# Two experts at fixed ranks, their weights issued before the ranking of the experts is known

## The chip, the cores and the metric

One core of one Trainium2 chip runs the whole program. The metric is the device time of one execution in microseconds (us). The kernel before took 2995.73 us (median of 3 runs, 2994.79 to 2996.75).

## The reference, cut to what matters

The program is two transformer blocks over 256 tokens of width 1024. The first has two layers of attention and a product-key expert lookup. The second mixes tokens with two recurrent mixers and ends in a mixture of experts (`_moe`), which is the only part that the change touches:

```
scores = sigmoid(xt @ w_router)                  # 256 tokens x 64 experts
biased = scores + bias;  keep the best 4 of 8 groups of 8 experts
sel = top_k(candidates, 8);  wts = scores[sel] / sum * 2.5
for each expert e, for the tokens that chose it:
    y += wts * ((silu(x @ w_gate[e]) * (x @ w_up[e])) @ w_down[e])
out = y + shared expert
```

There are 256 x 8 = 2048 assignments over 64 experts, 32 on average. Each expert has 3 MB of float32 weights: gate and up together are 1024 x 512, down is 256 x 1024.

## The kernel before, in words

All weights of all 64 experts are streamed through SBUF once, in 192 pieces of 1 MiB. An expert has three pieces: part 0 and part 1 are the two halves of gate and up, part 2 is down.

The experts are ranked by how many tokens chose them. VectorE builds a key (size x 64 plus 63 minus the number of the expert) and sorts the 64 keys with eight rounds of max8 and match-replace in `moe` (L1741 to L1746). From the sorted keys it makes the list of expert numbers, which is announced as `order` (L1751). An expert's rank decides how much room it gets: ranks 0 to 7 have 128 rows, ranks 8 to 31 have 64, ranks 32 to 63 have 32. Where a size is over its room, a flag is set (`over`, L1753 to L1757), and a second wave over the table `AGAIN` serves the rows that did not fit; without the flag every engine jumps over it.

`STEPS` (L249 to L258) is the first wave, 28 steps. A step fills the 128 rows of TensorE with one, two or four experts. Step 0 holds ranks 8 and 9, step 1 ranks 32 to 35, step 2 rank 0, step 3 ranks 10 and 11, and so on.

`PIECES` (L269) is the order of the 192 pieces: for each step s its part 0, its part 1, and then part 2 of the step before. So the order starts with step 0 part 0 (2 pieces), step 0 part 1 (2), step 1 part 0 (4), step 1 part 1 (4), step 0 part 2 (2), step 2 part 0 and part 1, step 1 part 2 (4), step 3 part 0. Below, piece n is the n-th of this order, counted from 0. There are 13 places in SBUF (`PLACES`); piece n goes to place n modulo 13.

SyncE issues the pieces, strictly in this order (`weights` in `sync_program`, L2652). It waits once for `order`, then reads each expert's number from the list with a value_load and issues the piece with a source address made from it. From piece 13 on it waits until the matmuls that used the place's former piece are done: `("used", "piece", step, part)` of piece n - 13. The first 13 have other conditions: pieces 0 to 5 wait for the last projection of the mixer, which was done long before, pieces 6 and 7 for the second half of the shared expert's up projection (`("ps", "shared", 1)`), pieces 8 and 9 for the end of the shared expert's down projection (`("used", "w_sh")`), and pieces 10 to 12 for the store of the token table. Ahead of piece 9 SyncE also issues the store of the shared expert's output to `y_tab`, and that waits for this output.

TensorE runs, in program order: router, shared up projection, sizes and ranks, tables of slots for 12 steps (`slots`), `shared_down`, and then `experts`. In `experts` (L956) the order is: up(0), turn(1), hidden(0); then for each s: up(s), one chunk of slot tables, turn(s+1), down(s-1), hidden(s). up(s) uses parts 0 and 1 of step s, down(s) uses part 2. So down(0) comes after up(1) and turn(2). GpSimd gathers the rows of each step from `x_tab` with one indirect DMA (L2502), and adds the results to `y_tab` with one indirect accumulating DMA per expert (L2514).

Of the kernel before, what the change touches and what calls it, by code (L numbers as in the profile page):

```python
# [5 lines left out]
P = 128  # L6
ALU = mybir.AluOpType
# [13 lines left out]
class Counts:  # L21
# [3 lines left out]
    def __init__(self):  # L25
        self.table, self.known = {}, False
# [134 lines left out]
def bc(a, axis, n):  # L161
    u = a.unsqueeze(axis)
    s = list(u.shape)
    s[axis] = n
    return u.to_broadcast(s)


def heads(a, n):
    return a.rearrange("p (h x) -> p h x", h=n)
# [79 lines left out]
def expert_steps():  # L249


    r = []
    for i in range(8):
        r += [(8 + 2 * i, 9 + 2 * i), tuple(range(32 + 4 * i, 36 + 4 * i)), (i,)]
    return r + [(24 + 2 * i, 25 + 2 * i) for i in range(4)]


STEPS = expert_steps()  # L258
CAPACITIES = ((0, 128), (8, 64), (32, 32))

AGAIN = [(r,) for r in range(32)] + [(8, 9)] + [tuple(range(32 + 4 * i, 36 + 4 * i)) for i in range(8)]
AGAIN_FROM = [128] * 8 + [64] * 24 + [192] + [32] * 8
WAVES = (STEPS, AGAIN)
FIRST = [[sum(len(x) for x in steps[:s]) for s in range(len(steps))] for steps in WAVES]
LAST_CHUNK = 6
PLACES = 13


PIECES = [[(t, part, i) for s in range(len(steps) + 1) for t, part in ((s, 0), (s, 1), (s - 1, 2))  # L269
           if 0 <= t < len(steps) for i in range(len(steps[t]))] for steps in WAVES]  # L270
PIECE_OF = [{x: n for n, x in enumerate(pieces)} for pieces in PIECES]


class MoeSide:


    def __init__(self, ar, modT, iu):
        two = lambda o, n: ar(o, n).rearrange("p (c n) -> p c n", c=2)
        self.Wt, self.sg, self.bi, self.Mk = (two(128 * i, 128) for i in range(4))
        self.g8, self.m8, self.kp = ar(512, 64), ar(576, 8), ar(584, 8)  # L280
        self.gsum, self.ssum, self.big = ar(592, 8), ar(600, 8), ar(608, 64)
        self.TW = ar(672, 256).rearrange("p (c e x) -> p c e x", c=2, x=2)
        self.RW, self.RWT, self.rkp = two(928, 256), two(1184, 256), two(1440, 128)
        self.Pm, self.key, self.order, self.rank, self.rev = (ar(1568 + 64 * i, 64) for i in range(5))
        self.ST = ar(1888, 128).rearrange("p (s x) -> p s x", x=2)
        self.ig, self.iy, self.colm = ar(2016, 64), ar(2080, 72), ar(2168, 1)
        self.OH = ar(2304, 2048).rearrange("p (c e s) -> p c e s", c=2, e=8)
        self.ysh = two(4352, 2048)
        self.xg = [ar(6400 + 1024 * i, 1024) for i in range(4)]
        self.XT, self.yb = ([ar(o + 1024 * i, 1024) for i in range(2)] for o in (10496, 12544))  # L290
        self.sgm, self.hid, self.hidT = ([ar(o + 256 * i, 256) for i in range(2)] for o in (14592, 15104, 15616))
        self.hsh = ar(15104, 512)
        self.sums = [two(6400, 2048), two(8448, 2048)]
        self.sh2 = modT[:, 24:32]
        self.row_of, self.add_to = iu[:, 0:64], iu[:, 64:132]
        self.digits, self.expert = iu[:, 192:256], iu[:, 256:320]


def build(nc, d, out):
    import numpy as np  # L300
    ctx = ExitStack()
    with ctx:
        def sb(name, n, dt=F32):
            return ctx.enter_context(nc.sbuf_tensor(name, [P, n], dt))
# [25 lines left out]
        iu = sb("iu", 512, U32)  # L330
# [4 lines left out]
        def tile_of(*name):  # L335

            return banks[where.get(name, 0)]
# [21 lines left out]
        def R(i, k):  # L359
            return ring[:, i * 1024:(i + k) * 1024]  # L360
# [18 lines left out]
        at = Counts()  # L379
# [25 lines left out]
        def piece(wave, *which):  # L405

            i = PIECE_OF[wave][which] % PLACES
            return R(2 * i, 2) if i < 10 else ar(16384 + 2048 * (i - 10), 2048)
# [7 lines left out]
        def tensor_program(pe):  # L416
# [451 lines left out]
            def moe():  # L868
# [81 lines left out]
                def slots_again():  # L950
                    b = fresh("slots", 1, 0, among=(0,))
                    for k, rs in enumerate(AGAIN):
                        one_hots(1, k, [k % 8], [k], [rs], b)
# [86 lines left out]
        def vector_program(v):  # L1040
# [660 lines left out]
            def moe():  # L1701
                m = moe_side
# [29 lines left out]
                for c in range(2):  # L1732
# [6 lines left out]
                          ("out", "rank", c))  # L1739
                    v.ts(m.RW[:, c, 0:64], m.RW[:, c, 0:64], 1000.0, None, ALU.add, None, ("RW", c))  # L1740
                v.stt(m.key, tile_of("sizes")[:, 0:64], 64.0, m.rev, ALU.mult, ALU.add, ("out", "sizes"))  # L1741
                for i in range(8):
                    o8 = m.order[:, 8 * i:8 * i + 8]
                    v.max8(o8, m.key)
                    if i < 7:
                        v.replace8(m.key, o8, m.key, -1.0)  # L1746
# [5 lines left out]
                v.ts(m.Pm, m.rank, m.colm, None, ALU.is_equal, None, ("permutation",))  # L1752
                for i, (rank, n) in enumerate(CAPACITIES):  # L1753
                    v.ts(m.ssum[:, i:i + 1], m.order[:, rank:rank + 1], 64.0 * (n + 1), None, ALU.is_ge, None)
                for i in (1, 2):
                    v.tt(m.ssum[:, 0:1], m.ssum[:, 0:1], m.ssum[:, i:i + 1], ALU.max)
                v.cp(flag[:, 0:1], m.ssum[:, 0:1], ("over",))  # L1757
                v.wait_ge(*at("ps", "by rank", 0))
# [14 lines left out]
                def rows(wave, g, o, n):  # L1773

                    part = slice(o, o + n)
                    v.wait_ge(*at("ps", "slots", wave, g))
                    v.cp(m.ST[:, part], tile_of("slots", wave, g)[:, 0:2 * n].rearrange("p (e x) -> p e x", x=2),
                         ("out", "slots", wave, g))
                    x, ig = m.ST[:, part, 0], m.ig[:, part]
                    v.ts(ig, x, 0.0, 1000.0, ALU.is_equal, ALU.mult)  # L1780
                    v.stt(ig, x, -1.0, ig, ALU.add, ALU.add)
                    v.cp(m.row_of[:, part], ig)
                    return ig

                sr = C("slot_rows")
# [22 lines left out]
                def slots_again():  # L1808
                    for k, (rs, first) in enumerate(zip(AGAIN, AGAIN_FROM)):
                        v.wait_ge(*(at("used", "onehot", 1, k - 8) if k > 7 else at("used", "onehot", 0, LAST_CHUNK)))  # L1810
                        by = len(rs)
                        for c in range(2):
                            o = m.OH[:, c, k % 8, :].rearrange("p (x s) -> p x s", x=by)
                            v.tt(o, bc(C("iota")[:, first:first + P // by], 1, by),
                                 bc(m.rkp[:, c, rs[0]:rs[0] + by], 2, P // by), ALU.is_equal, ("onehot", 1, k))
                    ig = rows(1, 0, 0, 41)
                    v.cp(m.iy[:, 0:32], ig[:, 0:32])
                    v.tt(m.iy[:, 32:34], sr[:, 0:2], ig[:, 32:33].to_broadcast([P, 2]), ALU.add)
                    v.tt(heads(m.iy[:, 34:66], 8), bc(ig[:, 33:41], 2, 4), bc(sr[:, 2:6], 1, 8), ALU.add)
                    v.cp(m.add_to[:, 0:66], m.iy[:, 0:66], ("slots", 1, 0))  # L1820

                def experts(wave, more):
                    steps = WAVES[wave]
# [59 lines left out]
                with v.e.If(over > 0):  # L1883
                    slots_again()
                    experts(1, iter(()))
                    v.wait_ge(*at("added", 1, len(AGAIN) - 1, 0))
                    v.fill(m.m8, 0.0)
# [667 lines left out]
        def sync_program(sp):  # L2555
# [89 lines left out]
            m = moe_side  # L2645
# [5 lines left out]

            def weights(wave, before):  # L2652

                sp.wait_ge(*at("order"))
                e = {}
                for n, (s, part, i) in enumerate(PIECES[wave]):
                    if wave == 0 and n == 9:
                        load(rows_of(y_tab[0:T, :]), m.ysh, s_tab, ("tables",),
                             after=[("out", "ysh", c, i) for c in range(2) for i in range(2)])
                    rank = WAVES[wave][s][i]  # L2660
                    if wave == 0 and n == 20:
                        load(hT_sb[:, 0:D], d["rows"][14:15, :].to_broadcast([P, D]), s_post, ("loaded", "ffn", "post"),
                             after=[("ps", "shared", 1)])
                    if part == 0:
                        e[rank] = sp.e.value_load(m.expert[0:1, rank:rank + 1], min_val=0, max_val=63) if at.known else 0
                    src = d["w_down"][bass.ds(e.pop(rank), 1), :, :] if part == 2 else \
                        d["w_gu"][bass.ds(e[rank], 1), :, 2048 * part:2048 * part + 2048]
                    old = [("used", "piece", wave, *PIECES[wave][n - PLACES][0:2])] if n >= PLACES else before(n)
                    load(piece(wave, s, part, i), src.rearrange("a p n -> (a p) n"), piece_sems[wave][n % PLACES],
                         ("loaded", "piece", wave, s, part, i), after=old)  # L2670
# [177 lines left out]
```

## Time and profile before

| | us |
|---|---|
| median of 3 runs | 2995.73 |
| the profiled execution, its own time | 2992.89 |
| span of the profiled execution | 2991.1 |
| first piece of expert weights issued | 2371.19 |
| last piece issued | 2925.00 |
| end of the span | 2991.1 |

Times inside the profile are us from the start of the span. The expert stage is the last 620 us. The page's line of DMA shares cuts the span in 40 slices of 74.8 us; slices 32 to 39 are this stage. PE is TensorE, DVE is VectorE, SP is SyncE.

### The profile page before, as it was taken

The numbers are of one execution on the slowest core, as the hardware profiler recorded it, in microseconds if no ns is written. First come the engines' busy times: TensorE is split into PE (matmuls) and PEld (weight loads), VectorE is DVE, ScalarE is ACT, GpSimd is POOL, SyncE is SP. The second block draws the span as 40 slices with busy tenths as digits, with TensorE's granted clock in tenths as the row PEclk, the third lists the DMA queues.
The fourth block names the chain that finished last, engine by engine and source line by source line (L and its number), as shares of the span: only waits on it lengthen the run. The fifth ranks groups of instructions, "written<-read, shape, count | busy, mean of one in ns | idle before, by whom it ended". The sixth has DMA issues, their size and how long they took to land.

```text
span 2991.1 us, 29479 instructions
## 1 busy us (share of the span) xinstructions
PE 2436.7 (81%) x9692; PEld 1331.3 (45%) x9692; DVE 1598.9 (53%) x3289; ACT 836.0 (28%) x2272; POOL 830.9 (28%) x723
## 2 busy tenths in 40 slices
PE   7898888888887988998897899789797786767673
PEld 3684333333333766344443455458783532222221
DVE  4556657485444636758889877556644521121111
ACT  1313333333332412343343444323110111111110
POOL 1004333343331102334444556112010112122221
PEclk9799999999999799999999999899998788888887
DMA  7029999999998126999898899612113399999994
GB/s 276 1 85 403 422 422 422 422 415 422 422 398 346 57 85 248 376 366 395 355 420 313 358 422 395 245 43 71 43 57 131 140 408 397 389 391 381 382 381 147
DMA packets 129843, 885.95 MB, mean 296 GB/s; under 512 B 23184, under 2 KB 23568, under 8 KB 31760
## 3 DMA queue, kind: packets, MB, share of 16 engines
q0 software_dynamic: 86976, 553.74, 46.0%
q1 hardware_dynamic: 42704, 330.22, 27.5%
q8 instruction: 79, 1.29, 0.2%
q14 instruction: 84, 0.69, 0.1%
HBM read 877.56 MB, written 37.75 MB: 306 GB/s over the span
## 4 chain that ended last, share of the span: by engine, by line
PE 46%; DMA 25%; DVE 20%; ACT 4%; issue 3%; SPq 1%; POOL 1%; DVEq 0%; ACTq 0%; POOLq 0%
PE ps L155 44%; DMA ring<-in_peer_uv,idx_u 11%; DMA ring<-in_w_gu 6%; DVE ring L1307 6%; DVE arena L76 5%; DMA ring<-in_w_down 3%; ACT arena L125 3%; PE ps L158 2%; DMA arena<-in_w_gu 2%; DMA arena<-in_w_down 1%; DVE arena L1307 1%; DVE iu L113 1%; DVE arena L109 1%; SPq L2560 1%; DVE arena L97 1%
## 5 line engine op out<-in xcount | busy, mean ns | idle before, releaser
L155 PE MATMUL ps<-ring,arena 128*128 128x512 f32 (+3 forms) x3264 | 1262.9, 653 | 281.2 <-ACT arena L125 159.9
L155 PEld LDWEIGHTS ps<-ring,arena 128*128 128x128 f32 (+2 forms) x3264 | 473.6, 180 | 957.3 <-issue 605.1
L1307 DVE CUSTOM_DVE_ANT_0 ring<-ring,h 128x1024 f32<-128x1024 f32 x448 | 563.0, 1257 | 328.3 <-DMA ring<-in_peer_uv,idx_u 294.9
L2377 POOL DMA_INDIRECT ring<-in_peer_uv,idx_u x448 | 491.5, 1097 | 754.8 <-PE ps L155 609.4
L155 PE MATMUL ps<-arena 128*128 128x128 f32 (+7 forms) x2504 | 502.8, 383 | 106.4 <-ACT arena L125 42.9
L125 ACT ACTIVATE arena<-arena 128x1 f32<-128x1 f32 (+4 forms) x1097 | 296.7, 270 | 747.6 <-DVE arena L1307 646.3
L155 PEld LDWEIGHTS ps<-arena 128*128 128x128 f32 (+3 forms) x2504 | 316.0, 193 | 263.5 <-issue 148.3
L76 DVE TENSOR_TENSOR arena<-arena,ps 128x512 f32<-128x512 f32 (+1 forms) x158 | 93.7, 593 | 446.9 <-ACT arena L125 358.6
L125 ACT ACTIVATE arena<-ps 128x512 f32<-128x512 f32 (+4 forms) x198 | 109.8, 554 | 774.1 <-PE ps L155 712.5
L155 PE MATMUL ps<-ring,hT 128*128 128x512 f32 (+2 forms) x896 | 307.0, 503 | 16.9 <-DVE hT L97 11.9
L125 ACT ACTIVATE arena<-cst,arena 128x128 f32<-128x128 f32 x512 | 205.5, 401 | 162.3 <-PE ps L155 122.0
L155 PEld LDWEIGHTS ps<-ring,hT 128*128 128x128 f32 x896 | 171.7, 198 | 141.2 <-issue 114.1
L2514 POOL DMA_INDIRECT y_tab<-arena,iu x64 | 100.1, 1564 | 435.5 <-DVE arena L97 309.6
L134 POOL TENSOR_TENSOR small<-small,cst 128x1 f32<-128x1 f32 (+3 forms) x42 | 46.6, 1109 | 534.4 <-DVE small L84 520.6
L155 PE MATMUL ps<-hT,ring 128*128 128x128 f32 (+1 forms) x1280 | 182.2, 306 | 12.0 <-ACT hT L125 12.0
L155 PEld LDWEIGHTS ps<-hT,ring 128*128 128x128 f32 x1280 | 171.1, 199 | 21.1 <-issue 10.5
L158 PE MATMUL ps<-cst,arena 128*128 128x128 f32 (+1 forms) x706 | 114.9, 313 | 57.4 <-DVE arena L76 29.0
L158 PEld LDWEIGHTS ps<-cst,arena 128*128 128x128 f32 (+1 forms) x706 | 94.3, 158 | 112.8 <-issue 45.5
L97 DVE COPY arena<-ps 128x512 f32<-128x512 f32 (+5 forms) x102 | 59.6, 584 | 149.9 <-PE ps L155 81.5
L134 POOL TENSOR_TENSOR arena<-arena,cst 128x512 f32<-128x512 f32 (+2 forms) x52 | 67.6, 1301 | 230.8 <-DVE arena L76 135.4
L2377 POOL DMA_INDIRECT arena<-in_peer_uv,idx_u x64 | 70.6, 1103 | 130.7 <-PE ps L155 128.2
L1307 DVE CUSTOM_DVE_ANT_0 arena<-arena,h 128x1024 f32<-128x1024 f32 x64 | 81.1, 1267 | 42.4 <-DMA arena<-in_peer_uv,idx_u 36.5
(117 smaller groups left out, 1486.6 us busy)
## 6 DMA issues: line engine op xcount, KB each, us to landing
ring<-in_w_gu SPq DMA_DIRECT2D x98, 1024.0 KB, 28.5
ring<-in_w_down SPq DMA_DIRECT2D x52, 1024.0 KB, 29.8
ring<-in_w_in SPq DMA_DIRECT2D x16, 2048.0 KB, 12.6
arena<-in_w_gu SPq DMA_DIRECT2D x30, 1024.0 KB
ring<-in_w_mod SPq DMA_DIRECT2D x12, 2048.0 KB
ring<-in_peer_wq SPq DMA_DIRECT2D x8, 2048.0 KB, 8.1
ring<-in_w_o SPq DMA_DIRECT2D x6, 2048.0 KB, 11.1
ring<-in_w_gates SPq DMA_DIRECT2D x12, 1024.0 KB, 4.9
```

The costliest lines, as they stand in the source:

```text
L76: self.done(self.e.tensor_tensor(o, a, b, op), *names)
L97: self.done(self.e.tensor_copy(o, a), *names)
L109: self.done(self.e.max(out=o, in_=a), *names)
L113: self.done(self.e.max_index(o, m, a), *names)
L125: self.done(self.e.activation(o, a, f, **k), *names)
L134: self.done(self.e.tensor_tensor(o, a, b, op), *names)
L155: return self.e.matmul(o, lhsT, rhs, start=start, stop=stop, skip_group_check=True)
L158: return self.e.transpose(o, src, ident)
L1307: v.done(v.e.tensor_tensor_reduce(out=row, in0=row, in1=h[:, n // 128, :], scale=1.0, scalar=0.0, op0=ALU.mult, op1=ALU.add, accum_out=aa[ ...
L2377: g.e.indirect_dma_start(out=landing(n), out_offset=None, in_=d["peer_uv"], in_offset=bass.IndirectOffsetOnAxis(ap=idx_u[:, n:n + 1], axis ...
L2514: g.e.indirect_dma_start(out=y_tab, out_offset=index(m.add_to, n), in_=m.yb[s % 2], in_offset=None, bounds_check=2 * T - 1, oob_is_err=Fal ...
L2560: sp.e.dma_start(o, src).then_inc(sem, 16)
```

## The change

Experts 0 and 1 get ranks 8 and 9 whatever their sizes, and the others are ranked around them. The first round of the sort sees key -1 for both; ahead of the second round their keys return, raised by 65536 and 32768, so that they come first among what is left. The raise does not touch the low six bits, from which the expert's number is read. The room check looks at rank 10 in place of rank 8, and at the larger size of the two fixed experts. The table of the second wave gets two more entries. SyncE issues the six pieces of step 0 with constant addresses and waits for `order` only ahead of the first piece whose expert it has to read. In `PIECES` part 2 of step 0 moves from behind step 1 to places 4 and 5 of the order. The list of places and the condition of each piece number stay as they are.

```diff
-CAPACITIES = ((0, 128), (8, 64), (32, 32))
+KNOWN = {8: 0, 9: 1}
+CAPACITIES = ((0, 128), (10, 64), (32, 32))
...
+PIECES[0] = PIECES[0][0:4] + [(0, 2, 0), (0, 2, 1)] + [x for x in PIECES[0][4:] if x[0:2] != (0, 2)]
 PIECE_OF = [{x: n for n, x in enumerate(pieces)} for pieces in PIECES]
...
+                v.cp(m.kp[:, 0:2], m.key[:, 0:2])
+                v.fill(m.key[:, 0:2], -1.0)
                 for i in range(8):
                     o8 = m.order[:, 8 * i:8 * i + 8]
+                    if i == 1:
+                        for e in range(2):
+                            v.ts(m.key[:, e:e + 1], m.kp[:, e:e + 1], 32768.0 * (2 - e), None, ALU.add, None)
                     v.max8(o8, m.key)
...
-                for i in (1, 2):
+                v.tt(m.ssum[:, 3:4], m.kp[:, 0:1], m.kp[:, 1:2], ALU.max)
+                v.ts(m.ssum[:, 3:4], m.ssum[:, 3:4], 64.0 * 65, None, ALU.is_ge, None)
+                for i in (1, 2, 3):
                     v.tt(m.ssum[:, 0:1], m.ssum[:, 0:1], m.ssum[:, i:i + 1], ALU.max)
...
             def weights(wave, before):
-                sp.wait_ge(*at("order"))
...
-                    if part == 0:
+                    known = wave == 0 and rank in KNOWN
+                    if known:
+                        which = slice(KNOWN[rank], KNOWN[rank] + 1)
+                    elif part == 0:
+                        sp.wait_ge(*at("order"))
                         e[rank] = sp.e.value_load(m.expert[0:1, rank:rank + 1], min_val=0, max_val=63) if at.known else 0
-                    src = d["w_down"][bass.ds(e.pop(rank), 1), :, :] if part == 2 else \
-                        d["w_gu"][bass.ds(e[rank], 1), :, 2048 * part:2048 * part + 2048]
+                    if not known:
+                        which = bass.ds(e[rank] if part < 2 else e.pop(rank), 1)
+                    src = d["w_down"][which, :, :] if part == 2 else d["w_gu"][which, :, 2048 * part:2048 * part + 2048]
                     old = [("used", "piece", wave, *PIECES[wave][n - PLACES][0:2])] if n >= PLACES else before(n)
```

The rest of the diff is in the second wave: `AGAIN` and `AGAIN_FROM` get the entries (10, 11) from row 192 and (32, 33, 34, 35) from row 64, and the index arithmetic of `slots_again` covers 43 entries in place of 41.

## Rows read from the trace of the kernel before

**Rows 1.** Page, DMA engines' share in tenths and GB/s, in 40 slices

```profile
DMA  7029999999998126999898899612113399999994
GB/s 276 1 85 403 422 422 422 422 415 422 422 398 346 57 85 248 376 366 395 355 420 313 358 422 395 245 43 71 43 57 131 140 408 397 389 391 381 382 381 147
```

**Rows 2.** Windows: stretch, length, busy us per engine, PEclk, DMA share, GB/s

```profile
2342.00:2371.00 29.00, 24.32 (x111) 21.30 (x109) 19.31 (x99) 7.36 (x14) 0.00 (x0) 0.81 0.13 53
2371.00:2379.00 8.00, 4.77 (x115) 4.19 (x114) 5.28 (x12) 0.60 (x1) 0.00 (x0) 0.87 0.82 310
2379.00:2396.00 17.00, 12.04 (x36) 6.49 (x38) 5.60 (x16) 2.70 (x6) 5.06 (x5) 0.76 1.01 418
2396.00:2422.00 26.00, 18.88 (x167) 7.50 (x165) 6.24 (x13) 2.27 (x6) 0.00 (x0) 0.85 1.02 416
2422.00:2434.00 12.00, 12.00 (x83) 5.63 (x78) 2.54 (x6) 2.19 (x5) 2.14 (x2) 0.75 1.01 416
2434.00:2464.00 30.00, 24.08 (x120) 10.77 (x122) 9.45 (x26) 5.15 (x12) 7.66 (x6) 0.91 1.02 400
2464.00:2925.00 461.00, 320.27 (x1508) 120.44 (x1500) 79.42 (x195) 56.61 (x132) 105.50 (x75) 0.84 0.99 386
```

**Rows 3.** Tiles in_w_gu, in_w_down: issue to landing, pieces 0, 3, 8, 13, all from 2429

```profile
DMA to landing us min/median/max: 5.1/5.1/5.1
...
DMA to landing us min/median/max: 11.5/11.5/11.5
...
DMA to landing us min/median/max: 9.2/9.2/9.2
...
DMA to landing us min/median/max: 19.3/19.3/19.3
...
DMA to landing us min/median/max: 17.3/29.4/34.1
```

**Rows 4.** Timeline of SP: start, us, line, tiles, count; pieces 0 to 9, 17, 25

```profile
2341.57 0.38 SPq L2560 DMA_DIRECT2D y_tab<-arena  x1
2371.19 2.68 SPq L2560 DMA_DIRECT2D ring<-in_w_gu  x4
...
2374.64 3.63 SPq L2560 DMA_DIRECT2D ring<-in_w_gu  x4
...
2392.84 0.33 SPq L2560 DMA_DIRECT2D ring<-in_w_gu  x1
2393.41 0.38 SPq L2560 DMA_DIRECT2D y_tab<-arena  x1
2393.98 0.33 SPq L2560 DMA_DIRECT2D ring<-in_w_gu  x1
...
2415.46 0.85 SPq L2560 DMA_DIRECT2D ring<-in_w_down  x2
...
2430.10 0.34 SPq L2560 DMA_DIRECT2D arena<-in_w_gu  x1
```

**Rows 5.** Timeline of DVE and POOL around the sort, and the first gathers

```profile
2355.57 0.17 DVE L76 TENSOR_TENSOR arena<-arena 128x8 f32<-128x8 f32 x1
2355.78 0.17 DVE L109 MAX8 arena<-arena 128x8 f32<-128x8 f32 x1
2356.02 0.06 DVE L101 MEMSET arena<- 128x4 f32 x1
2371.50 0.15 DVE L97 CAST flag<-arena 128x1 uint32<-128x1 f32 x1
2372.01 0.62 DVE L97 COPY arena<-ps 128x128 f32<-128x128 f32 x2 [0.36 <-PE ps L155]
...
2383.22 1.08 POOL L2502 DMA_INDIRECT arena<-x_tab,iu  x1 [41.68 <-DVE arena L76]
2387.22 0.99 POOL L2502 DMA_INDIRECT arena<-x_tab,iu  x1 [0.30 <-issue]
```

**Rows 6.** Chain that ended last: start, us, what; shared_down, up(0), up(1), down(0), down(1)

```profile
2384.00 8.68 PE ps L155 x16
...
2395.19 7.10 PE ps L155 x32
...
2408.89 9.85 PE ps L155 x64
...
2424.55 5.36 PE ps L155 x16
...
2443.88 4.27 PE ps L155 x32
...
2449.85 24.32 DMA ring<-in_w_gu
...
2915.58 30.23 DMA ring<-in_w_down
```

More of the change, by code:

```diff
@@ L258 @@
 STEPS = expert_steps()
-CAPACITIES = ((0, 128), (8, 64), (32, 32))
-AGAIN = [(r,) for r in range(32)] + [(8, 9)] + [tuple(range(32 + 4 * i, 36 + 4 * i)) for i in range(8)]
-AGAIN_FROM = [128] * 8 + [64] * 24 + [192] + [32] * 8
+KNOWN = {8: 0, 9: 1}
+CAPACITIES = ((0, 128), (10, 64), (32, 32))
+AGAIN = [(r,) for r in range(32)] + [(8, 9), (10, 11)] + \
+    [tuple(range(32 + 4 * i, 36 + 4 * i)) for i in range(8)] + [(32, 33, 34, 35)]
+AGAIN_FROM = [128] * 8 + [64] * 24 + [192] * 2 + [32] * 8 + [64]
 WAVES = (STEPS, AGAIN)
@@ L294, in __init__ @@
         self.sh2 = modT[:, 24:32]
-        self.row_of, self.add_to = iu[:, 0:64], iu[:, 64:132]
+        self.row_of, self.add_to = iu[:, 0:64], iu[:, 64:136]
         self.digits, self.expert = iu[:, 192:256], iu[:, 256:320]
@@ L1815, in slots_again @@
                                  bc(m.rkp[:, c, rs[0]:rs[0] + by], 2, P // by), ALU.is_equal, ("onehot", 1, k))
-                    ig = rows(1, 0, 0, 41)
+                    ig = rows(1, 0, 0, 43)
                     v.cp(m.iy[:, 0:32], ig[:, 0:32])
-                    v.tt(m.iy[:, 32:34], sr[:, 0:2], ig[:, 32:33].to_broadcast([P, 2]), ALU.add)
-                    v.tt(heads(m.iy[:, 34:66], 8), bc(ig[:, 33:41], 2, 4), bc(sr[:, 2:6], 1, 8), ALU.add)
-                    v.cp(m.add_to[:, 0:66], m.iy[:, 0:66], ("slots", 1, 0))
+                    v.tt(heads(m.iy[:, 32:36], 2), bc(ig[:, 32:34], 2, 2), bc(sr[:, 0:2], 1, 2), ALU.add)
+                    v.tt(heads(m.iy[:, 36:72], 9), bc(ig[:, 34:43], 2, 4), bc(sr[:, 2:6], 1, 9), ALU.add)
+                    v.cp(m.add_to[:, 0:72], m.iy[:, 0:72], ("slots", 1, 0))
                 def experts(wave, more):
```

## The prediction

> **What bounds the kernel now.** I read the page's DMA line first. The reader is to see that the slices of the expert stage stand at 9 up to the last one, at 381 to 408 GB/s, where the best slices of the whole span reach 422 [rows 1]. The table of windows says the same more closely. From 2379 to 2925 the DMA share is 0.99 to 1.02 in every stretch; from 2342 to 2371 it is 0.13 [rows 2]. Then I read how long pieces take from issue to landing. A piece issued to idle DMA engines, piece 0, lands after 5.1 us; from 2429 on none lands in under 17.3 us, and the median is 29.4 [rows 3]. Each piece thus stands in a queue behind others, and the stream of 192 pieces never runs dry from 2371 until the last is issued. The chain of waits looks different until 2449.85: it runs through TensorE and VectorE (shared_down, up(0), up(1), down(0), down(1)), and only then through DMA, in links of 24 to 30 us [rows 6]. That does not contradict it. TensorE's chain sets when places come free, the stream sets when data come, and both are tight to 2449. After that the stream alone decides. So I treat the end as: start of the stream, plus its work, plus every gap in which it has nothing issued, plus a tail that the change does not touch: 2991.1 less the last landing, 2915.58 + 30.23 = 2945.8, or 45.3 us [rows 6].
>
> **The unit.** A piece is 1.049 MB, at 422 GB/s 2.49 us [rows 1]. A stream that starts anew lands its first piece 5.1 us after issue [rows 3], so its work begins 5.1 - 2.5 = 2.6 us after issue.
>
> **Removed from the stream: 6 pieces.** Pieces 0 to 5 of the new order have constant addresses and no wait but the mixer's, long met. SyncE issues them right behind the store of zeros at 2341.57 [rows 4]. They need 6 x 2.49 = 14.9 us, and DMA is nearly idle until 2371 [rows 2]; they are done by about 2362. Their cover is whole. **-14.9 us.**
>
> **Added ahead of `order`.** A copy, a fill and two additions on VectorE, each in the dependent chain. A small tensor_tensor starts 0.21 us before what follows it; a fill is 0.06 us busy [rows 5], 0.09 with the same step to the next. 3 x 0.20 + 0.09 = 0.7 us. Piece 6, the first that waits for `order`, is issued at 2371.19 + 0.7 = 2371.9. **+0.7 us** to the start of the remaining stream. Three more small operations stand before the flag, 0.6 us. VectorE had waited 0.36 us for TensorE at 2372.01 [rows 5]; 0.7 + 0.6 - 0.36 = 0.95, so the slot tables, the gathers, shared_down, up(0) and all of TensorE's chain to down(1) come 0.95 us later. The two value_loads fewer are worth nothing. Their wait on `order` now stands ahead of piece 6; nothing behind it in SyncE's queue was to run sooner.
>
> **Gap A, ahead of piece 8.** Only pieces 6 and 7 follow `order` at once. Piece 8 waits by its number for the end of shared_down: 2384.00 + 8.68 = 2392.7, issued at 2392.84 [rows 4, 6]. Before, eight pieces covered that wait. Now two do. They are ready at 2371.9 + 2.6 + 2 x 2.49 = 2379.5. Piece 8 is issued at 2393.8 and its work begins at 2396.4. Of these 16.9 us the four gathers from 2383 [rows 5] fill some: piece 3 landed at 2373.4 + 11.5 = 2384.9, piece 8 at 2402.0 [rows 3, 4], 17.1 us for five pieces of 2.49, so 4.7 us were the gathers'. The gap is 16.9 - 4.7 = 12.2 us. By bytes alone the gathers could be near 3 us, which would make it 14. **+12.2 us.**
>
> **Gap B, ahead of piece 17.** This is the step I take to decide the sign. With part 2 of step 0 at places 4 and 5, piece 17 needs the place of piece 4, which is free only after down(0). In the old order piece 17 waited for up(1) part 0 and went out at 2415.46; the one that waited for down(0) was piece 25, at 2430.10, and its 8.6 us of waiting stood over a full queue [rows 4]. SyncE issues in order, so all behind piece 17 wait too, though up(1) frees eight places at 2415 to 2420. The stream meanwhile holds pieces 8 to 16 and the table store, ten units: 2396.4 + 24.9 + 1.4 for the fifth gather = 2422.7. The 1.4 is what is left from piece 8 (2402.0) to piece 13 (2399.0 + 19.3 = 2418.3) over six units [rows 3]. Piece 17 is issued at 2430.10 + 0.95 = 2431.05 and its work begins at 2433.7. **+11.0 us.** I looked for a third gap and find none: pieces 17 to 28 go out by about 2438, twelve units, to 2465 and beyond, and piece 29 needs down(1), which ends near 2449 [rows 6]. Piece 13 (now the last of up(1) part 1) lands at 2396.4 + 7 x 2.49 + 1.4 = 2415.2, some 0.5 us ahead of its use; if late, it adds its lateness to gap B, up to 2 us.
>
> **The sum.** -14.9 + 0.7 + 12.2 + 11.0 = +9.0 us. The profiled execution took 2992.89 us for a span of 2991.1, 2.8 us under the median of the runs, 2995.73; I add the sum to the median: 3004.7 us. Bounds: gap A 11 to 14, gap B 9 to 13, the shift of the chain 0.5 to 1.5 (it counts in B only), the removed pieces 14.4 to 15.5 at the rates of the windows (400 to 422 GB/s, 2.62 to 2.49 us a piece). That gives +5.5 to +13.
>
> The second wave costs nothing: the reference's routing with its own inputs gives expert 0 48 tokens and expert 1 16, both under 65, 59 at new rank 10 and 24 at new rank 32. No size is over its room, so the longer second wave is jumped over.
>
> **A page of the skill beside a row.** The row shows 5.1 us for a fresh 1 MiB piece, 2.6 beyond its transfer [rows 3]. The Trainium skill, "DMA: Bandwidth & Descriptors", section "Anatomy of one DMA", fits a transfer as 2.0 us plus bytes / 436e3, measured for the GpSimd path. By it a piece is 2.40 us and a fresh start 2.0; the gaps become 12.4 and 11.8, the removed work 14.4, and the sum is +10.5 in place of +9.0. I keep the rows.
>
> **Rivals.**
> (1) The full gain: the six pieces leave a stream that stays full. -14.9 + 0.7 = -14.2, 2981.5 us, faster. For it: the DMA share of 0.13 before 2371 and 1.0 behind it [rows 2]. Against: the stream stays full only if something else is issued from 2379 to 2396 and from 2422 to 2434. It decides where the two gaps together are under 14.2 us; I have 23.2.
> (2) Gap A alone: piece 17 is issued in time, because down(0) comes early or the queue is longer than I count. +9.0 - 11.0 = -2.0, 2993.7 us, no measurable change. Against: down(0) starts at 2424.55 by TensorE's own order, not for want of data (its weights had landed by 2418.3).
> (3) The first steps are TensorE's: the chain to 2449 is the bound and what the stream does before then is hidden. Only the added VectorE work is left, +1, 2996.7 us. For it: the chain of waits [rows 6]. Against: at 2449.85 the stream has pieces queued 24 us deep, so a delay in it is not absorbed but handed on.
> (4) A room is exceeded and the second wave runs: 216 pieces more at 389 GB/s, over 580 us. The sizes exclude it here.
>
> **Chances.** Forecast 0.70, rival 1 0.06, rival 2 0.12, rival 3 0.08, rival 4 0.01, a larger loss than +13 0.03. About 0.2% (6 us) is what a measurement of this kernel can tell from no change. Slower by more: most of the forecast's range and the larger losses, 0.66. Within: rivals 2 and 3 and the low end of the forecast, 0.27. Faster: 0.07. The forecast's own range is 3001 to 3009; the range for 8 in 10 reaches down to rivals 2 and 3, 2994 to 3009.
>
> **What would show it.** Right: six issues of in_w_gu and in_w_down between 2342 and 2346; a DMA share near 1 to about 2360, near 0 until 2372; in 2380 to 2396 a share of 0.2 to 0.4; the issue that was at 2415.46 now at about 2431, and a share well under 1 between 2423 and 2433; the wait of PE for in_w_gu that ended at 2463 ending at about 2470; and 45.3 us of tail as before. Wrong: a share near 1 from 2396 through 2434 (then rival 2 or 3), six issues that start only behind `order`, or any issue behind the last gather (a second wave).

## The result, and the profile after

| | us | ratio to before |
|---|---|---|
| before (6 runs) | 2995.86 | |
| changed kernel (6 runs, 3003.15 to 3010.67) | 3006.92 | 1.0038, 95% interval 1.0027 to 1.0050 |
| changed kernel again, later, 5 runs | 3007.64, beside 2994.26 | 1.0046, 1.0032 to 1.0059 |

The change makes the kernel slower by 11 to 13 us in the medians. The forecast was +9.0 us, 3004.7, with a range of +5.5 to +13; the first result lies inside it, the second (+13.4) just above.

The page of the kernel after: the DMA share and GB/s in 40 slices of 75.0 us. The expert stage is slices 32 to 39, as in [rows 1]; the reader is to see 342 in slice 32 where [rows 1] has 408, and no other slice of this stage more than 5 under it.

```profile
DMA  6029999999997126999898999502122589999994
GB/s 275 1 85 407 422 422 421 422 415 422 422 399 327 57 85 272 375 375 396 355 421 317 363 416 402 201 29 85 43 74 99 196 342 402 395 384 385 380 381 142
```

In this execution the stage began 3.73 us earlier than in the profiled execution of before: the store of zeros stands at 2337.84, not 2341.57. So I compare times from this store. The windows of the kernel after (length, busy us per engine, PEclk, DMA share, GB/s), to be laid beside [rows 2]:

```profile
2342.00:2371.00 29.00, 22.38 (x111) 19.76 (x110) 20.95 (x109) 4.54 (x9) 0.00 (x0) 0.86 0.62 240
2371.00:2379.00 8.00, 6.48 (x112) 6.32 (x112) 3.55 (x8) 0.00 (x0) 0.00 (x0) 0.50 0.50 202
2379.00:2396.00 17.00, 12.59 (x34) 5.75 (x36) 5.16 (x14) 2.70 (x6) 5.07 (x5) 0.77 0.49 139
2396.00:2422.00 26.00, 19.09 (x157) 8.47 (x157) 6.24 (x13) 2.27 (x6) 0.00 (x0) 0.78 0.94 386
2422.00:2434.00 12.00, 12.00 (x86) 5.72 (x82) 2.54 (x6) 2.19 (x5) 2.24 (x2) 0.76 0.23 84
2434.00:2464.00 30.00, 24.23 (x113) 11.10 (x112) 7.63 (x23) 4.47 (x11) 7.60 (x6) 0.89 1.02 394
2464.00:2935.00 471.00, 316.74 (x1514) 118.64 (x1514) 81.21 (x200) 57.42 (x133) 105.52 (x75) 0.83 0.99 387
```

The early loads are there: share 0.62 from 2342 to 2371, where it was 0.13. Both gaps are there too: 0.49 from 2379 to 2396 and 0.23 from 2422 to 2434, where [rows 2] has 1.01 in both. From 2434 on the stream is full again and stays so up to 2935.

The timeline of SP in the kernel after, as in [rows 4] (the last two lines are pieces 8 and 17 by themselves, from narrower windows):

```profile
2337.84 0.38 SPq L2573 DMA_DIRECT2D y_tab<-arena  x1
2338.26 3.94 SPq L2573 DMA_DIRECT2D ring<-in_w_gu  x4
2342.25 1.06 SPq L2573 DMA_DIRECT2D ring<-in_w_down  x2
2368.13 23.81 SPq L2573 DMA_DIRECT2D ring<-in_w_gu  x3
2401.72 29.64 SPq L2573 DMA_DIRECT2D ring<-in_w_down  x4
...
2391.60 0.33 SPq L2573 DMA_DIRECT2D ring<-in_w_gu  x1
...
2429.99 0.33 SPq L2573 DMA_DIRECT2D ring<-in_w_down  x1
```

Six pieces go out in 5 us behind the store. Pieces 6 and 7 follow `order` at 2368.13, piece 8 comes 22 us later. Pieces 16 to 19 stand in one line of 29.64 us: 16 at 2401.72, and 17 only at 2429.99.

How long pieces 7, 8, 16 and 17 took from issue to landing in the kernel after, as in [rows 3]:

```profile
DMA to landing us min/median/max: 6.9/6.9/6.9
...
DMA to landing us min/median/max: 6.1/6.1/6.1
...
DMA to landing us min/median/max: 19.9/19.9/19.9
...
DMA to landing us min/median/max: 4.9/4.9/4.9
```

Piece 17 landed in 4.9 us, piece 0 of before in 5.1: both found the DMA engines idle or nearly so. Piece 16 landed at 2401.7 + 19.9 = 2421.6. Piece 17 landed at 2434.9, so its work, 2.5 us, began at about 2432.4. So gap B was 10.8 us.

The chain that ended last in the kernel after, shared_down, up(0), up(1), down(0), down(1), and its first and last links through DMA, as in [rows 6]:

```profile
2381.77 9.66 PE ps L155 x16
...
2393.94 7.10 PE ps L155 x32
...
2409.26 9.54 PE ps L155 x64
...
2424.60 5.21 PE ps L155 x16
...
2443.92 4.12 PE ps L155 x32
...
2450.58 34.86 DMA ring<-in_w_gu
...
2924.02 30.56 DMA ring<-in_w_down
2954.58 2.55 issue
2957.13 5.22 PE ps L155 x16
```

Down(0) starts 86.8 us behind the store of zeros; in [rows 4, 6] it was 83.0. The piece in the chain's last link through DMA is piece 188, the fourth from the end. It lands 616.7 us behind the store, before 604.2: +12.5 us. From its landing to the end of the span, here called the tail, it is 46.5 us, before 45.3.

### The profile page after: what moved, and what is told of

Same layout as the page of the kernel before. It is cut to its first block, busy times and chain, and to the rows that moved or that the text cites. A ratio compares the mean times of both kernels' runs of the same rounds, so it can differ in the third digit from the quotient of the medians.

```text
span 3001.1 us, 29468 instructions
## 1 busy us (share of the span) xinstructions
PE 2429.2 (81%) x9692; PEld 1327.0 (44%) x9692; DVE 1601.1 (53%) x3296; ACT 836.3 (28%) x2272; POOL 833.8 (28%) x723
## 4 chain that ended last, share of the span: by engine, by line
PE 43%; DMA 27%; DVE 21%; ACT 4%; issue 3%; SPq 1%; POOL 1%; DVEq 0%; ACTq 0%; POOLq 0%
PE ps L155 41%; DMA ring<-in_peer_uv,idx_u 13%; DMA ring<-in_w_gu 6%; DVE ring L1313 6%; DVE arena L76 5%; ACT arena L125 3%; DMA ring<-in_w_down 3%; PE ps L158 2%; DMA arena<-in_w_gu 2%; SPq L2573 1%; DVE arena L109 1%; DVE arena L1313 1%; DVE iu L113 1%; DVE arena L97 1%; DMA arena<-in_w_down 1%
## 5 line engine op out<-in xcount | busy, mean ns | idle before, releaser
L155 PE MATMUL ps<-arena 128*128 128x128 f32 (+7 forms) x2504 | 492.7, 380 | 118.9 <-ACT arena L125 48.6
L155 PEld LDWEIGHTS ps<-hT,ring 128*128 128x128 f32 x1280 | 170.3, 199 | 20.6 <-issue 10.5
L1313 DVE CUSTOM_DVE_ANT_0 arena<-arena,h 128x1024 f32<-128x1024 f32 x64 | 81.1, 1267 | 44.1 <-DMA arena<-in_peer_uv,idx_u 38.2
```

The costliest lines, as they stand in the source:

```text
L155: return self.e.matmul(o, lhsT, rhs, start=start, stop=stop, skip_group_check=True)
L1313: v.done(v.e.tensor_tensor_reduce(out=row, in0=row, in1=h[:, n // 128, :], scale=1.0, scalar=0.0, op0=ALU.mult, op1=ALU.add, accum_out=aa[ ...
```

## The experiments

Each kernel from the change again to e10 ran beside the kernel before (e2, e5 and the change again 5 times, the others 11 times, before 21 or 27 times); the first row of the change is the result above. "Stage" is the time from the store of zeros to the end in the one profiled execution of each kernel; it leaves out the part ahead of the stage, where the change adds nothing and which put the store anywhere from 2337.8 to 2344.2. The last column has the issues, in us after the store.

| kernel | median, before beside it | ratio, 95% interval | stage | piece 8, piece 17 after the store |
|---|---|---|---|---|
| before | 2995.86 | | 649.5 | 51.3, 73.9 |
| the change | 3006.92, 2995.86 | 1.0038, 1.0027 to 1.0050 | 663.3 | 53.8, 92.2 |
| the change again | 3007.64, 2994.26 | 1.0046, 1.0032 to 1.0059 | 663.3 | 53.8, 92.3 |
| e1 fixed ranks only | 2993.75, 2994.11 | 0.9997, 0.9988 to 1.0006 | 649.4 | 53.5, 77.4 |
| e2 order only | 3006.65, 2994.11 | 1.0044, 1.0030 to 1.0058 | 659.2 | 51.4, 90.1 |
| e3 early, old order | 2994.65, 2994.11 | 1.0001, 0.9992 to 1.0010 | 652.4 | 53.8, 77.7 |
| e4 places by release | 2995.42, 2994.11 | 1.0002, 0.9993 to 1.0011 | 650.9 | 53.5, 77.5 |
| e5 gap A closed | 3008.34, 2994.85 | 1.0047, 1.0033 to 1.0061 | 662.8 | 32.5, 92.2 |
| e6 both | 2991.30, 2994.85 | 0.9987, 0.9978 to 0.9996 | 647.0 | 32.3, 77.7 |
| e7 old order, arena places | 2989.88, 2994.85 | 0.9983, 0.9974 to 0.9992 | 646.3 | 33.9, 77.7 |
| e8 before, arena places | 2993.19, 2994.85 | 0.9995, 0.9986 to 1.0004 | 649.5 | 36.8, 73.9 |
| e9 e7, flag late | 2990.45, 2994.26 | 0.9988, 0.9979 to 0.9997 | 641.9 | 34.2, 74.0 |
| e10 e9, store late | 2988.72, 2994.26 | 0.9982, 0.9973 to 0.9991 | 643.9 | 33.9, 74.2 |

**e1, fixed ranks only.** The changed kernel with the old order of pieces and the wait for `order` ahead of all.

```diff
-PIECES[0] = PIECES[0][0:4] + [(0, 2, 0), (0, 2, 1)] + [x for x in PIECES[0][4:] if x[0:2] != (0, 2)]
...
             def weights(wave, before):
+                sp.wait_ge(*at("order"))
```

> The fixed ranks alone: VectorE's added operations stay, but SyncE waits for the list of experts before it issues anything, and the pieces stand in the old order. Stream theory: the start of the stream moves by 0.7 us and no gap opens, so +0.7 to +1.5 us against the kernel before, with a DMA share of 1 from 2373 to the end. Rival (the longer VectorE and TensorE chain is the loss, since shared_down came 2.5 us and down(0) 3.8 us later in the changed kernel, counted from the store of zeros): +4 us or more, up to the whole +11.

Measured: no difference, 0.9997. Piece 17 went out 3.5 us later than before, counted from the store, and it cost nothing, since the stream had work queued. The windows of e1, laid where [rows 2] has them, show the share at 1 throughout:

```profile
2379.00:2396.00 17.00, 13.36 (x37) 7.47 (x37) 4.95 (x15) 1.48 (x3) 4.08 (x4) 0.67 1.00 411
2396.00:2422.00 26.00, 20.63 (x138) 8.94 (x138) 4.66 (x12) 3.11 (x9) 0.99 (x1) 0.80 1.01 398
2422.00:2434.00 12.00, 9.14 (x96) 4.59 (x93) 4.70 (x10) 2.58 (x6) 0.00 (x0) 0.72 1.01 419
```

The rival, that the longer chain on VectorE and TensorE is the loss, falls.

**e2, order only.** The kernel before with one line.

```diff
+PIECES[0] = PIECES[0][0:4] + [(0, 2, 0), (0, 2, 1)] + [x for x in PIECES[0][4:] if x[0:2] != (0, 2)]
```

> The kernel before with nothing but the new order of pieces (part 2 of step 0 at places 4 and 5). Stream theory: piece 17 waits for down(0), which itself comes some 3.7 us later because up(1) part 1 now needs piece 13 (2418.3) instead of piece 11 (2413.3); the stream runs dry at about 2426 and starts again at about 2436, +10 us. Rival (the loss is in the VectorE operations or in the early loads): 0 us.

Measured: 1.0044, about +12.5 us in the medians and +9.7 in the stage. Nothing is loaded early here and no operation is added. This one line alone brings a loss like that of the change in the medians; in the stage it brings 9.7 of the 13.8 us. The timeline of SP in e2, with piece 17:

```profile
2433.70 1.36 SPq L2561 DMA_DIRECT2D ring<-in_w_down  x3
```

The windows of e2, the second one ahead of that issue:

```profile
2398.00:2424.00 26.00, 19.96 (x137) 8.56 (x132) 4.01 (x9) 2.13 (x6) 0.00 (x0) 0.80 1.01 413
2424.00:2436.00 12.00, 9.44 (x96) 5.00 (x97) 4.77 (x10) 2.33 (x6) 0.84 (x1) 0.86 0.22 81
```

Piece 17 goes out at 2433.70, and the share ahead of it is 0.22. The delay of down(0) that I expected, 3.7 us, was 1.6 (90.1 us from the store, piece 25 of before 88.5).

**e3, early loads in the old order.** The change without the same line; four pieces go early.

```diff
-PIECES[0] = PIECES[0][0:4] + [(0, 2, 0), (0, 2, 1)] + [x for x in PIECES[0][4:] if x[0:2] != (0, 2)]
```

> The change with the old order of pieces: four pieces are issued early, part 2 of step 0 stands behind step 1 again. Stream theory: 4 pieces leave the stream (-9.9 us), its start moves by 0.7, gap A opens at about 8.7 us (pieces 4 to 7 done at 2384.5, gathers 4.7, piece 8 begins at about 2397.9), gap B is gone: -0.5 us against before, within -3 and +2. Rival (what is loaded early is gained in full): -9 us. Rival (VectorE chain): still +4 or more.

Measured: 1.0001, as expected. Ten us of transfers were made early and nothing came of it. Gap A took them: the share from 2379 to 2396 was 0.58.

**e4, places by release.** The change with the place of a piece from 13 on chosen by which place is freed first.

```diff
+FREED = [[(t, part, i) for s in range(len(steps) + 1) for t, part in ((s, 0), (s, 1), (s - 1, 2))
+          if 0 <= t < len(steps) for i in range(len(steps[t]))] for steps in WAVES]
+START = [list(range(PLACES)), list(range(PLACES))]
+PLACE_OF = [{}, {}]
+for w in range(2):
+    for n, x in enumerate(PIECES[w]):
+        PLACE_OF[w][x] = START[w][n] if n < PLACES else PLACE_OF[w][FREED[w][n - PLACES]]
...
-                    old = [("used", "piece", wave, *PIECES[wave][n - PLACES][0:2])] if n >= PLACES else before(n)
+                    old = [("used", "piece", wave, *FREED[wave][n - PLACES][0:2])] if n >= PLACES else before(n)
```

> The change as it is, with one thing taken away: from piece 13 on a piece takes the place that was freed first, so piece 17 takes a place of step 1 part 0 and waits for up(1) part 0, not for down(0). Stream theory: gap B goes, gap A (now about 13.7 us) stays, -14.9 + 0.7 + 13.7 = -0.5 us against before, so some 11 us faster than the change. Rival (VectorE chain or early loads make the loss): +9 to +11, no better than the change.

Measured: 1.0002, so some 11 us faster than the change, as expected. Here are e4's windows. Gap A is open (0.31), gap B is gone (1.02), while e4 still has all six early loads and all added operations:

```profile
2379.00:2396.00 17.00, 13.68 (x39) 7.96 (x38) 4.49 (x13) 1.20 (x2) 4.08 (x4) 0.65 0.31 97
2396.00:2422.00 26.00, 20.30 (x136) 8.90 (x138) 5.12 (x13) 3.40 (x9) 0.99 (x1) 0.80 0.99 386
2422.00:2434.00 12.00, 9.14 (x99) 4.31 (x92) 4.34 (x9) 2.06 (x6) 0.00 (x0) 0.72 1.02 422
```

**e5, gap A closed, gap B left.** The other lines are those of e4, with `FREED = PIECES`, so that from piece 13 on the places go round as in the change.

```diff
+START = [[0, 1, 2, 3, 4, 5, 6, 7, 10, 11, 12, 8, 9], list(range(PLACES))]
...
-                    if wave == 0 and n == 9:
+                    if wave == 0 and n == 11:
...
-                    [("ps", "shared", 1)] if n < 8 else [("used", "w_sh"), ("used", "router bias")] if n < 10 else [("x stored",)])
+                    [("ps", "shared", 1)] if n < 8 else [("x stored",)] if n < 11 else [("used", "w_sh"), ("used", "router bias")])
```

> The change with gap A mostly closed and gap B left: the three places in the arena, free since the store of the token table, are used for pieces 8 to 10, the two places of the shared expert's weights for 11 and 12, and the store of the shared expert's output stands ahead of piece 11. Stream theory: piece 17 still goes out at down(0), whatever the stream did before, so what gap A gives back gap B takes: within 2 us of the change, some +10 us against before. Rival (the two gaps add up independently, as my sum of four terms reads when its terms are taken one by one): about 8 us faster than the change, +2 against before.

Measured: 1.0047, no better than the change (1.0038 and 1.0046); the gain of 8 us that the rival expected is excluded. Piece 8 went out 21 us earlier and piece 17 at the same 92.2 us. The windows of e5 show the work taken from behind (share 0.65 from 2401, 0.18 from 2427):

```profile
2384.00:2401.00 17.00, 12.11 (x32) 5.58 (x34) 5.57 (x16) 2.70 (x6) 5.06 (x5) 0.75 0.68 245
2401.00:2427.00 26.00, 19.19 (x132) 8.22 (x128) 6.19 (x13) 2.27 (x6) 0.00 (x0) 0.79 0.65 263
2427.00:2439.00 12.00, 11.90 (x99) 5.86 (x100) 2.58 (x7) 2.19 (x5) 1.75 (x2) 0.74 0.18 68
```

**e6, both mended** (the diffs of e4 and e5 together), and **e7, the diff of e5 in the old order.**

> Both mended at once: places by release (no gap B) and the arena places for pieces 8 to 10 (gap A from 13.7 us to about 6.3). Stream theory: -14.9 + 0.7 + 6.3 = -7.9 us against before, faster than both kernels. Rival (what is early is hidden by TensorE's chain up to 2449 anyway): -1 to +1 us against before.

> Early loads and fixed ranks, old order of pieces (four early), arena places for pieces 8 to 10. Stream theory: -9.9 + 0.7 + 1.3 (pieces 4 to 10 and the gathers done at 2396.6, piece 11 begins at about 2397.9) = -7.9 us against before, the same as the kernel with six early and both gaps mended, because in both 11 pieces are in before the shared expert's places come free. Rival (each piece loaded early counts): 5 us less than that kernel's gain.

Measured: 0.9987 and 0.9983, by these ratios 3.9 and 5.1 us faster than before, and faster than the change by 15 us or more. That is less than the 7.9 us expected. The two are equal within their intervals, as expected of kernels that both hold 11 pieces when the shared expert's places come free. The windows of e7 show what is missing (the last three cut the stretch more finely):

```profile
2377.00:2394.00 17.00, 13.69 (x38) 7.80 (x38) 4.61 (x14) 1.19 (x2) 4.07 (x4) 0.65 0.93 382
2394.00:2420.00 26.00, 20.31 (x139) 8.84 (x138) 4.99 (x13) 3.39 (x9) 0.99 (x1) 0.80 0.81 316
...
2391.00:2397.00 6.00, 4.36 (x21) 2.14 (x22) 2.06 (x5) 2.10 (x5) 0.99 (x1) 1.00 0.66 249
2397.00:2413.00 16.00, 11.95 (x82) 6.26 (x82) 4.02 (x9) 1.89 (x5) 0.00 (x0) 0.78 1.01 405
2413.00:2420.00 7.00, 7.00 (x56) 1.96 (x48) 0.00 (x0) 0.00 (x0) 0.00 (x0) 0.77 0.36 128
```

A share of 0.81 over 26 us is 4.9 us without work, where I had left 1.3. There are two gaps, and I had looked at the first alone. Ahead of piece 11 some 2.0 us are empty (a share of 0.66 over 6 us): it went out 54.9 us after the store, behind the store of the shared expert's output, not at 53.8. The larger one, 4.5 us (0.36 over 7 us), stands ahead of piece 17, which waits for up(1) part 0 and is issued at 2417.26, 77.7 us after the store. With more loaded early, the stream has run out by then. e6 has the same second gap. (The first of the three windows begins 3 us ahead of the 26 us, so the two sums differ.)

**e8, the kernel before with the diff of e5.**

> The kernel before with the arena places for pieces 8 to 10 and nothing else. Stream theory: the stream of before has no gap at piece 8, so 0 us, within 1.5. Rival (the other use of the places is itself the gain of the two kernels beside it): -3 us or more.

Measured: 0.9995, no difference that can be told; the stage is 649.5 us in both. The use of the places is no gain by itself.

**e9 and e10.** e9 is e7 with the nine operations of the flag (the expectation counts ten) behind the shared expert's hidden product; e10 also with `n == 13` for the store of the shared expert's output.

```diff
-                for i, (rank, n) in enumerate(CAPACITIES):
-                    v.ts(m.ssum[:, i:i + 1], m.order[:, rank:rank + 1], 64.0 * (n + 1), None, ALU.is_ge, None)
...
                 v.tt(m.hsh, m.hsh, m.ysh[:, 1, 0:512], ALU.mult, ("hidden", "shared"))
+                for i, (rank, n) in enumerate(CAPACITIES):
+                    v.ts(m.ssum[:, i:i + 1], m.order[:, rank:rank + 1], 64.0 * (n + 1), None, ALU.is_ge, None)
...
```

> The kernel with the old order and arena places for pieces 8 to 10, and beside it the flag of the second wave computed later: its ten small VectorE operations stand behind the shared expert's hidden product, under shared_down, and no longer ahead of the slot tables. In that kernel the stream still ran dry before piece 11, which waits for shared_down. Stream theory: shared_down ends 1.5 to 2.5 us earlier (ten operations at 0.2 us, less the 0.7 us until TensorE's by-rank product is there), piece 11 too, and the time falls by as much, to about -7 us against before. Rival (the remaining gap is not what bounds it): no change against that kernel's -5.

> The same, and the store of the shared expert's output stands behind pieces 11 and 12 instead of ahead of them, so that piece 11 goes out when shared_down's last product is done, 1.1 us earlier than behind the store (which waits for the copies out of PSUM). Stream theory: another -1 us, about -8 against before. Rival: no change.

Measured: 0.9988 and 0.9982, that is 3.6 and 5.4 us under before where about 7 and 8 were expected. Against e7's 0.9983 neither can be told apart in the whole time, so the rivals (no change) stand. The issues moved as expected: in e9 piece 11 goes out at 52.5 us after the store for 54.9 and piece 17 at 74.0 for 77.7, in e10 piece 11 at 51.6 and piece 17 at 74.2. Of e7's two gaps the first is gone in e9 and some 2.8 us are left of the second (a share of 0.60 over 7 us). The profiled stages are 4.5 and 2.4 us shorter than e7's, one execution each; that e10's is the longer of the two is not what was expected. Whether any of it shows in the whole time is left open. e10 has the lowest median measured, 5.4 us under before by its ratio (2.7 to 8.1), though its interval overlaps those of e6, e7 and e9.

**The change again.**

> The changed kernel as it is, beside the others on one chip. Its first six runs gave +11.1 us against before with a spread of 7.5 us. In the profiled execution the expert stage alone, from the store of zeros to the end, was 13.8 us longer and what comes before it 3.7 us shorter. Stream theory with gap B: the stage is 13 to 14 us longer again; what comes before it is the same code and varies either way, so +11 to +14 in the median. If the 3.7 us belong to the change: again some 3 to 4 us shorter before the stage.

Measured: +13.4 us, and a stage of 663.3 us, the same to 0.1 us as in the first profile. The store of zeros stood at 2342.43, so the 3.7 us of the first profile do not belong to the change.

## Why the prediction was right, point by point

- **The bound is the stream of pieces.** Right. A line that left the stream without work for 10 us made most of the loss by itself (e2), and delays on TensorE with a full queue cost nothing (e1).
- **Six pieces removed, under full cover.** Right: issued from 2338.26 to 2343.3, share 0.62 until 2371. That the removal is real is seen in e4, which pays for gap A and ends level.
- **Operations ahead of `order`, +0.7 us.** Right: 30.29 us from the store to piece 6, before 29.62 to piece 0.
- **The shift of TensorE's chain, 0.95 us.** This is the term that was mis-sized. Piece 8 came 2.5 us later, down(0) 3.8, piece 17 went out 92.15 us after the store where the forecast had 2431.05 - 2341.57 = 89.48. VectorE's part was as computed: the slot tables' first products start 1.00 us later, counted from the store. TensorE ran slower behind it: shared_down starts 1.50 us later and takes 9.66 us, before 8.68 [rows 6]. The windows of TensorE (length, busy us, granted clock, DMA share, GB/s) over the ten us that begin 42 us after the store, first of the kernel before and of the change:

```profile
2383.57:2393.57 10.00, 9.55 (x24) 0.82 1.02 421
...
2379.84:2389.84 10.00, 8.07 (x13) 0.65 0.50 153
```

Then of e9, which has the nine flag operations moved away:

```profile
2384.50:2394.50 10.00, 9.41 (x24) 0.82 0.99 408
```

The granted clock is 0.65 in the change against 0.82, that is, more of the time at 1.2 GHz and less at 2.4. Cut in windows of 2 us, it goes from 0.50 to 1.00 about 3 us into shared_down before and in e9, about 5 us into it in the change. In the change TensorE had waited 3.12 us for VectorE ahead of the slot tables, in e9 2.25 and before 2.26. e1 and e7, with the operations in the chain, show 0.66 and 0.63 too. A second loss follows: the 42 small products between up(0) and up(1) took 1.84 + 2.40 us, before 1.12 + 1.31. In both kernels the clock falls back to 0.50 about 66 us after the store; before, these products were through by then, in the change they begin there. So down(0) comes 3.8 us later and not 2.5.
- **Gap A, 12.2 us.** Piece 7 landed at 2376.2 and piece 8's work began at 2395.2: 19.0 us between them, less the 4.7 that the prediction took for the gathers is 14.3 (in the change the gathers' transfers fill about 5.0 us of the 16 DMA engines, so 4.7 was a fair term). Of the 2.1 us more, 1.5 are piece 8's later issue, behind the late shared_down. But the term was wrong in kind: e5 shows that it did not count by itself in the change. Piece 17 goes out at the end of down(0), whatever was done before. The time lost is where piece 17's issue stands, and my sum came out near it because its terms add up to just that. The profiles bear this out over all kernels in which piece 17's landing was recorded: it landed 78.8 us after the store in e9, 79.0 in e10, 82.5 in e6 and e7, 86.0 in e4, 86.1 in e3, 87.1 in e1, 94.9 in e2 and 97.1 in the change, and the stage was 562 to 566 us longer than that in each.
- **Gap B, 11.0 us.** Right: 10.8, and it decides the sign, as e2 and e4 show from both sides. That the size is so near is in part luck, since both of its ends came some 2.5 us later than forecast: the stream ran dry 83.8 us after the store for 81.1, and piece 17's work began at 94.6 for 92.1.
- **The tail, 45.3 us.** The prediction took the landing of 2945.8 for the last one. It is piece 188's; three more follow, and piece 190 landed at 2950.75, in the change at 2959.52. In the difference this cancels: piece 190 is 12.5 us later too, counted from the store. The tail was 46.5 us, not as before: the products that follow piece 188 took 5.22 us for 3.65, at a granted clock of 0.72 for 1.00. And "after that the stream alone decides" hides something. The windows just ahead of the last recorded landings, before (2950.75) and in the change (2962.01), from TensorE's view (length, busy us, clock, share, GB/s):

```profile
2943.00:2951.00 8.00, 4.96 (x26) 1.00 0.07 24
...
2953.00:2961.00 8.00, 4.97 (x18) 0.79 0.06 25
```

A share of 0.06 is one sixteenth. By my estimate from it, one DMA engine of the 16 still worked on the last pieces while the others had done their parts; which one, and why, is not shown.
- **The whole.** From 9.0 forecast: +2.7 for piece 17's issue gives 11.7; piece 188 landed +12.5, 0.8 more that I cannot place; the tail was 1.2 us longer. Together 13.7, and the stage is 13.8 longer (663.3 less 649.5), which is above the forecast's range; the medians, +11.1 and +13.4, have intervals that hold it. The bounds of the four terms, added up, give +5.2 to +13.3; the prediction wrote +5.5 to +13.
- **The signs.** They came as written but for two. The share of 0.2 to 0.4 in 2380 to 2396 was 0.49 (2379 to 2396), and the tail is the one above. TensorE's wait for in_w_gu that was to end at about 2470 ended at 2470.68, but in a stage that began 3.7 us earlier.
- **Rivals.** Rival 1 (the full gain) fails by the shares; even e6 and e7 keep only 4 to 5 us of the 14. Rival 2 (gap B not there) is not the change but is e4, which came at +0.6 us by its ratio (-2.1 to +3.3), where I had computed -2.0. Rival 3 (TensorE's chain hides the stream until 2449) is excluded by e2. Rival 4, the second wave, did not run: SyncE issued 192 pieces behind the store of zeros and no more.
- **The Trainium skill's fit** ("DMA: Bandwidth & Descriptors", "Anatomy of one DMA"), made for transfers of the GpSimd path and not for SyncE's, gave an estimate of +10.5 by 2.0 us for a fresh start. Piece 17 landed 4.9 us after issue, 2.4 beyond its 2.5 of transfer, between the page's 2.0 and my 2.6. The larger sum was nearer for another reason, the late down(0).

## What to carry to other kernels

When a kernel lives on a stream with a fixed number of places, a transfer made earlier only helps if the stream does not run dry afterwards: count what can still be issued until the next place comes free. Moving a piece forward whose place is freed late makes a later piece, and in an in-order queue all behind it, wait for that place; give places out in the order in which they are freed, not in which they are filled. Gaps in front of one fixed release do not add: find the last release ahead of which the stream runs dry, and measure from it. Closing one gap can open another behind it, as ahead of piece 17 in e6 and e7.

## What the runs showed of the hardware

- With VectorE operations of some 1.3 us more in all ahead of short TensorE work, the 16 matmuls of shared_down took 9.66 us for 8.68, at a granted clock of 0.65 for 0.82 over the ten us around them. In e1, where the stream stayed full, piece 17 went out 3.5 us later, though the slot tables' products had moved by only 1.2 us. Moving nine operations away took the whole shift back (e9: 74.0 us against 73.9 before). All profiles agree: 0.80 to 0.82 without these operations ahead of the slot tables (before, e2, e8, e9, e10), 0.63 to 0.66 with them. Why the clock rises later there is not shown.
- The part ahead of the stage, to which the change adds nothing, ended between 2337.8 and 2344.2 us, a spread as large as many of the effects. The stage's own length was 649.4 to 649.5 us in before, e1 and e8, and 663.3 twice in the change. It comes from one profiled execution of each kernel, and it does not always agree with the medians (e3: 2.9 us longer than before, at a ratio of 1.0001).
- The last weights landed with the DMA share at 0.06 to 0.07, at 24 to 25 GB/s, against 422 GB/s where the share is 1.
